# Dilated attention issued for pairs of heads, with their score and value products alternating between the two halves of the TensorE array

## What is computed

```
q, k = rope(a @ w_q[pattern]), rope(a @ w_k[pattern]);  v = a @ w_v[pattern]
s = q k^T / 8, masked to keys of the same residue and inside the window
o_pattern = softmax(s) v;   lse_pattern = max(s) + log(sum(exp(s - max)))
o = sum over the patterns of softmax(lse)_pattern * o_pattern
m = concat(o over the heads) @ w_o
```

## Time and profile before

| | us |
|---|---|
| median of 3 runs | 902.57 |
| lowest and highest run | 902.10, 903.83 |
| span of the profiled execution | 901.5 |
| TensorE busy in it | 873.2 (97%) |
| VectorE busy | 536.8 (60%) |
| ScalarE busy | 473.9 (53%) |
| GpSimd busy | 60.0 (7%) |
| attention of group 0, from its first score matmul to the next stage's first matmul | 41.4 |
| attention of group 1, the same | 41.3 |

### The profile page before, as it was taken

The page is one execution under the profiler, slowest core; times in us unless marked ns, Lnnn a source line. Parts: engine busy times, 40 slices in busy tenths (PEclk is TensorE's granted clock), DMA queues, the critical chain, the costliest instruction groups (busy, mean ns, idle before and its releaser), DMA issues. The chain is left out here.

```text
span 901.5 us, 12726 instructions
## 1 busy us (share of the span) xinstructions
PE 873.2 (97%) x4345; PEld 710.1 (79%) x4345; DVE 536.8 (60%) x1119; ACT 473.9 (53%) x819; POOL 60.0 (7%) x134
## 2 busy tenths in 40 slices
PE   6999999999999999989999999999999999999995
PEld 5898666778888888778887888888788788888874
DVE  5878776587645545685555535545555865555533
ACT  7676666665444444455445544445554644444331
POOL 3000038020000000110000000000001100000002
PEclk9999999999999999999999999999999999999998
DMA  7666100454656456347555015555204376645611
GB/s 251 206 203 222 47 2 1 140 165 157 217 187 222 150 189 226 98 151 241 178 182 158 1 48 173 184 168 187 82 1 141 118 232 199 220 154 188 217 47 48
DMA packets 90107, 135.20 MB, mean 150 GB/s; under 512 B 6304, under 2 KB 55504, under 8 KB 90064
## 3 DMA queue, kind: packets, MB, share of 16 engines
q1 hardware_dynamic: 89392, 132.53, 45.9%
q0 software_dynamic: 576, 2.10, 0.7%
q10 hardware_dynamic: 96, 0.02, 0.0%
HBM read 133.59 MB, written 1.05 MB: 149 GB/s over the span
## 5 line engine op out<-in xcount | busy, mean ns | idle before, releaser
L948 DVE TENSOR_TENSOR w_lo<-w_raw,w_hi 128x1024 fp32r<-128x1024 f32 x248 | 301.3, 1246 | 111.5 <-ACT w_hi L524 107.7
L1377 PE MATMUL ps<-w_hi,xt_hi 128*128 128x512 f32 x784 | 314.5, 401 | 2.1 <-DVE xt_lo L978 1.9
L1377 PE MATMUL ps<-w_hi,xt_lo 128*128 128x512 f32 x784 | 307.4, 392 | 0.0
L1377 PE MATMUL ps<-w_lo,xt_hi 128*128 128x512 f32 x784 | 306.9, 391 | 0.0
L524 ACT ACTIVATE w_hi<-w_raw 128x1024 fp32r<-128x1024 f32 x248 | 252.2, 1054 | 42.5 <-DMA w_raw<-in_ffn_w_gu 19.6
L1377 PEld LDWEIGHTS ps<-w_hi,xt_hi 128*128 128x128 f32 x784 | 148.4, 189 | 32.4 <-DVE xt_lo L978 2.7
L1377 PEld LDWEIGHTS ps<-w_hi,xt_lo 128*128 128x128 f32 x784 | 148.3, 189 | 31.4
L1377 PEld LDWEIGHTS ps<-w_lo,xt_hi 128*128 128x128 f32 x784 | 148.7, 190 | 28.3
L776 ACT ACTIVATE st_hi<-ps 128x256 fp32r<-128x256 f32 x44 | 16.8, 383 | 112.6 <-PE ps L1386 112.6
L1377 PE MATMUL ps<-w_hi,st_hi 128*128 128x512 f32 x176 | 69.0, 392 | 2.9 <-DVE st_lo L1240 2.8
L502 POOL TENSOR_TENSOR h<-h,tmp 128x512 f32<-128x512 f32 x16 | 24.1, 1527 | 714.6 <-DVE tmp L1216 714.6
(11 more groups left out here) (176 smaller groups left out, 825.5 us busy)
## 6 DMA issues: line engine op xcount, KB each, us to landing
w_raw<-in_ffn_w_gu SPq DMA_DIRECT2D x88, 512.0 KB, 4.7
w_raw<-in_dil_w_in SPq DMA_DIRECT2D x72, 512.0 KB, 4.0
w_raw<-in_ffn_w_down SPq DMA_DIRECT2D x44, 512.0 KB, 4.0
w_raw<-in_nsa_w_in SPq DMA_DIRECT2D x20, 512.0 KB, 4.6
w_raw<-in_nsa_w_o SPq DMA_DIRECT2D x8, 512.0 KB, 4.4
w_raw<-in_dil_w_o SPq DMA_DIRECT2D x8, 512.0 KB, 4.0
w_raw<-in_nsa_cmp_wk SPq DMA_DIRECT2D x4, 512.0 KB, 5.2
w_raw<-in_nsa_cmp_wv SPq DMA_DIRECT2D x4, 512.0 KB, 4.0
```

The lines of the kernel that those rows point to most:

```text
L948: dve.tensor_tensor(w_lo[:, n.slot, c:c + 1024], w_raw[:, n.raw, c:c + 1024], w_hi[:, n.slot, c:c + 1024].bitcast(F32), ALU.subtract)\
L1377: ins = pe.matmul(o, s, m, start=start, stop=stop)
```

## The change

Units are walked in pairs: pair t of a group is the units w = 16 hg + 2t (even head) and 16 hg + 2t + 1 (odd head) of the same half m = t % 2, where j = 2 (t // 2) + odd. A unit's number therefore stands for another head and half than before. The three score matmuls and the four value matmuls of the two units are issued alternately, even then odd, each still two instructions. The transposes are not interleaved. The order on the three engines becomes, for step t of eight pairs:

```diff
+        def pair_units(hg, t):
+            return 16 * hg + 2 * t, 16 * hg + 2 * t + 1
...
 ScalarE
-                for s in range(16 + 4):
-                    if 3 <= s < 19:
-                        pt_evac(1, 16 * hg + s - 3, 512)
-                    if s < 16:
-                        exp_unit(1, 16 * hg + s, 512, 1)
-                    if hg == 1 and s in (1, 5, 14):
+                for t in range(8 + 2):
+                    if t >= 2:
+                        for w in pair_units(hg, t - 2):
+                            pt_evac(1, w, 512)
+                    if t < 8:
+                        for w in pair_units(hg, t):
+                            exp_unit(1, w, 512, 1)
+                    if hg == 1 and t in (0, 2, 7):
...
 VectorE
-                for s in range(16 + 1):
-                    if s < 16:
-                        mask_unit(1, 16 * hg + s, 512, [mask_dil[:, s % 2, :]])
-                    if s >= 1:
-                        norm_unit(1, 16 * hg + s - 1, 512, [None])
-                    if hg == 1 and s in (2, 6, 15):
+                for t in range(8 + 1):
+                    if t < 8:
+                        for w in pair_units(hg, t):
+                            mask_unit(1, w, 512, [mask_dil[:, t % 2, :]])
+                    if t >= 1:
+                        for w in pair_units(hg, t - 1):
+                            norm_unit(1, w, 512, [None])
+                    if hg == 1 and t in (1, 3, 8):
...
 TensorE
-            def scores_dil(hg, u):
-                j, m, w = u // 2, u % 2, 16 * hg + u
-                if w >= 3:
-                    pe.wait_ge(masked[1], w - 2)
+            def scores_pair_dil(hg, t):
+                m, ws = t % 2, pair_units(hg, t)
+                for w in ws:
+                    if w >= 3:
+                        pe.wait_ge(masked[1], w - 2)
                 for pat, c, k0, n in ((0, 0, 0, S), (1, 256, m * P, P), (2, 384, m * P, P)):
-                    ins = pe.matmul(bank(score_bank(w), c, n), qk(pat, 0, j, m * P, P), qk(pat, 1, j, k0, n),
-                                    start=True, stop=True)
-                ins.then_inc(scores[1], 1)
+                    for odd, w in enumerate(ws):
+                        j = t // 2 * 2 + odd
+                        ins = pe.matmul(bank(score_bank(w), c, n), qk(pat, 0, j, m * P, P),
+                                        qk(pat, 1, j, k0, n), start=True, stop=True)
+                        if pat == 2:
+                            ins.then_inc(scores[1], 1)
...
+            def pv_pair_dil(hg, t):
+                m, ws = t % 2, pair_units(hg, t)
+                if (hg, t) == (1, 4):
+                    pe.wait_ge(ot_ready[1], 1)
+                pe.wait_ge(pt_out[1], ws[1] + 1)
+                c = ot_bank(hg, t // 4) * 512 + t // 2 % 2 * S + m * P
+                for k, (pat, mk) in enumerate(((0, 0), (0, 1), (1, m), (2, m))):
+                    for odd, w in enumerate(ws):
+                        j = t // 2 * 2 + odd
+                        ins = pe.matmul(view(ps, c, [[1, P]], p0=DH * odd, n=DH),
+                                        v_dil[:, pat, mk, j * DH:(j + 1) * DH],
+                                        p_t[:, w % 4, P * k:P * k + P], start=k == 0, stop=k == 3)
+                if t % 4 == 3:
                     ins.then_inc(pv_done[1], 1)
...
-                for s in range(16 + 5):
-                    if s < 16:
-                        scores_dil(hg, s)
-                    if 3 <= s < 19:
-                        turn_probs(1, 16 * hg + s - 3, 4)
-                    if s >= 5:
-                        pv_dil(hg, s - 5)
+                for t in range(8 + 3):
+                    if 2 <= t < 10:
+                        for w in pair_units(hg, t - 2):
+                            turn_probs(1, w, 4)
+                    if t < 8:
+                        scores_pair_dil(hg, t)
+                    if t >= 3:
+                        pv_pair_dil(hg, t - 3)
```

More of the change, by code:

```diff
@@ L915, in _ @@
                     dil_proj(hg, it + k, Piece(N_DIL + 18 * hg + 6 * k + AHEAD, it))
-                for s in range(16 + 4):
-                    if 3 <= s < 19:
-                        pt_evac(1, 16 * hg + s - 3, 512)
-                    if s < 16:
-                        exp_unit(1, 16 * hg + s, 512, 1)
-                    if hg == 1 and s in (1, 5, 14):
-                        ot_dil(*{1: (0, 0), 5: (0, 1), 14: (1, 0)}[s])
+                for t in range(8 + 2):
[6 more added lines that the diff above has]
+                    if hg == 1 and t in (0, 2, 7):
+                        ot_dil(*{0: (0, 0), 2: (0, 1), 7: (1, 0)}[t])
             ot_dil(1, 1)
@@ L1357, in _ @@
                     dve.wait_ge(dilmask_ready, 1)
-                for s in range(16 + 1):
-                    if s < 16:
-                        mask_unit(1, 16 * hg + s, 512, [mask_dil[:, s % 2, :]])
-                    if s >= 1:
-                        norm_unit(1, 16 * hg + s - 1, 512, [None])
-                    if hg == 1 and s in (2, 6, 15):
-                        ot_dil(*{2: (0, 0), 6: (0, 1), 15: (1, 0)}[s])
+                for t in range(8 + 1):
[6 more added lines that the diff above has]
+                    if hg == 1 and t in (1, 3, 8):
+                        ot_dil(*{1: (0, 0), 3: (0, 1), 8: (1, 0)}[t])
             ot_dil(1, 1)
@@ L1803, in pv_dil @@
-            def pv_dil(hg, u):
-                j, m = u // 2, u % 2
-                if (hg, u) == (1, 8):
-                    pe.wait_ge(ot_ready[1], 1)
[L1807 to L1812, removed]
+            def scores_pair_dil(hg, t):
[3 more added lines that the diff above has]
+                        pe.wait_ge(masked[1], w - 2)
+                for pat, c, k0, n in ((0, 0, 0, S), (1, 256, m * P, P), (2, 384, m * P, P)):
+                    for odd, w in enumerate(ws):
[4 more added lines that the diff above has]
+                            ins.then_inc(scores[1], 1)
```

## The result

The changed kernel takes 897.42 us (median of 5 runs, 895.89 to 900.11) against 902.91 us of the kernel before beside it: ratio 0.9943, 95% interval 0.9928 to 0.9959. The prediction was 894.4, range 891.5 to 898.5. The profiled execution has a span of 894.2 us (predicted 893.3); its time of 895.89 us is the shortest of the five, so the spans differ by 7.3 us where the medians differ by 5.5.

A forecast was written before the change was run, and what follows sets the result against it. TensorE bounds the kernel before; afterwards a closed wait of 4.48 us per pair makes each attention stage 37.3 us, not 41.4. Saving 8.2 from 901.5 gives span 893.3; the median lies 1.07 above, 894.4, range 891.5 to 898.5.

The forecast's parts named there:

- Bound now: Kernel before: TensorE, busy 873 of 901.5 us, bounds it; nothing waits long for VectorE or ScalarE.
- Do the halves overlap?: Attention scores and values: row halves and column halves run at full rate side by side while both have work queued.
- The first rival: Attention stages: halves don't overlap in this order; 3.7 us per stage more than before, median 910; chance 8%.
- the second, that only row halves overlap: Attention values: a pair's products don't overlap and take 1.89 us; median 899.6; chance 5%.
- TensorE per pair: Attention loop: transposes 1.02, scores 1.07 and values 1.02 us, together 3.1 against 5.36 before.
- The new wait: Attention loop: TensorE's transposes wait for norms queued behind both masks of the next pair; 4.48 us per pair.
- the chain: Attention loop: closed circle of scores, two masks, two norms, transposes, next scores; 4.48 us per pair against 5.36.
- mask to mask: VectorE: time from a pair's first mask to its second, taken as 0.77 us within the 4.48 us period.
- The clock: TensorE's 1.4 us pause per pair leaves the clock up; at 1.2 GHz the median would be about 920, chance 2%.
- the granted clock at 1.00: Attention stages: sign that the prediction is right, TensorE's granted clock staying at 1.00 despite its pauses.
- the sum for the stage: One attention stage, first score matmul to next stage's first matmul: 37.3 us against 41.4, with six periods of 4.48.
- Behind the stage: Projections after an attention stage keep TensorE busy 104.7 of 105.6 us, so saved time isn't lost waiting for weights.

The follow-up runs named there:

- e4: Kernel before, with VectorE doing norm(s-1) ahead of mask(s): 905.52 us, ratio 1.0016 to the kernel before.
- e7: Changed kernel, VectorE doing norms of pair t-1 before masks of pair t, and the value products not alternated: 881.95 us, ratio 0.9749 to the kernel before.
- e1: Changed kernel, with VectorE doing the norms of pair t-1 before the masks of pair t: 876.15 us, ratio 0.9691 to the kernel before.
- e3: Changed kernel plus 14 identity transposes in each of steps 2 and 3 of each group, filling TensorE's pauses: 894.28 us, ratio 0.989 to the kernel before.
- e6: Changed kernel with the pauses of steps 2 and 3 filled by identity transposes and scores and values not alternated: 895.39 us, ratio 0.9899 to the kernel before.
- e2: Changed kernel with the alternation of scores and values undone, even head's instructions before the odd head's: 902.87 us, ratio 0.9989 to the kernel before.
- e8: Changed kernel measured again, unedited: 897.39 us, ratio 0.9926 to the kernel before.
- e9: Changed kernel plus 14 identity transposes in step 2 of each group only, filling the first pause: 893.57 us, ratio 0.9903 to the kernel before.
- e10: Changed kernel plus 14 identity transposes in step 3 of each group only, filling the second pause: 896.04 us, ratio 0.9916 to the kernel before.

## Why the prediction was right, and where it was off

**Bound now.** Right. TensorE was full before, and e4 shows that an earlier norm bought nothing there.

**Do the halves overlap?** Right, read from three bursts of the trace before. Twelve scores in 1.15 us and sixteen values in 1.09 are the whole of it. The first rival (no overlap in this order, slower) falls with that. So does the second, that only row halves overlap: sixteen value products, which all use the 128 rows, last no longer than eight. Even in e7, with the values of a pair in order, 16 took 1.58 us and not 1.96. The Trainium skill's page "TensorE: Matmul & The Clock Gate", Part 3, "What overlaps and what doesn't", lets a weight load overlap running matmuls only when its row group differs; for these float32 products the traces disagree.

**TensorE per pair.** 3.1 predicted, 3.13 in e1, the only run that shows it. In the changed kernel it doesn't set the period.

**The new wait.** Right as a mechanism, and e1 shows it: opening the chain and nothing else brings the period from 4.32 to 3.13. The chain's length was forecast at 4.48. The mis-sized term is mask to mask: 0.77 by the one place in the earlier trace rows where two masks follow each other, but the second one waited there for its scores, which end at about 491.47 + 1.14 + 0.87 = 493.48 (an estimate from the earlier trace rows), and it starts at 493.50. Working without a pause it is 0.61 to 0.62 (509.87, 510.49, 511.10). Twelve periods at 0.16 too much are 1.9 us.

**The clock.** This is the step that failed, and with it the sign "the granted clock at 1.00": the stages had 0.91 and 0.95. The prediction took the pause of the steady loop, 1.4 us, set it beside 1.01 us ahead of the stage, let the clock stay, and gave the fall 2%, as a case in which it would be at 1.2 GHz throughout. It didn't look at the steps in which the value products, the cover named for the pause, do not exist yet: there the pause is 2.0 us, and the clock falls for a few us at a time, twice in group 0's stage of the profiled execution and once in group 1's. By e3 that costs 3.1 us of the median and most of the scatter. In the steady loop of pairs, with 0.97 us of pause, no profiled execution has the beginning of a fall, so that half of the argument held. That the length of the pause decides is not shown, as the last section says; that filling these two pauses keeps the clock up is.

The two errors have opposite signs. With the period at 4.32 a stage would have come to 37.3 - 6 x 0.16 = 36.3 us, and e3, the changed kernel without falls, has 36.2 twice: the sum for the stage is then right to 0.1 us. The forecast of the whole would have been 894.4 - 1.9 = 892.5, and its range, moved along, would have ended at 896.6. The measured 897.4 lies outside that. So the mechanism was right, but that the measured time fell inside the range is in part luck: the period, too long by 0.16, made room for the clock that had been left out. As it stands, the forecast is 3.0 us short, the gain 5.5 and not 8.2 us. (The 1.07 us between span and median belong to two different executions. In every run on record the time lies 1.7 to 1.8 us above the span of the same run.)

**Behind the stage.** Right: the projections take 105.7 us, TensorE is full in them, and nothing was given back, nor behind group 1.

**What the name of the change suggests.** I ascribed the gain to pairs and alternation together and didn't part them. The experiments do, with the queues in the order of this change. At full clock the walk in pairs alone gains 902.7 - 895.4 = 7.3 us (e6) and the alternation 1 to 2 more (e3). With the clock as it is, pairs alone gain nothing that could be told from none (e2), so that all of the measured 5.5 us hang on the alternation; most of what it gives there is that the clock stays low for a shorter time.

## What to carry to other kernels

When work is regrouped into larger steps, write down for each engine what stands in front of what in its queue, and follow the circle: a faster engine is worth only what the longest circle lets through, and one exchange of two independent blocks in another engine's queue (here 21 us, 3 of them by the clock) may be worth more than the change itself. The same exchange in the kernel before, which had no such circle, bought nothing (e4). If two engines wait for each other and both have idle time, look for such an exchange before anything else. Look at the first and last steps of a pipeline by themselves, since what covers a wait in the middle isn't there at the ends.

## What was not expected of the hardware

- Pauses of 2.0 us in TensorE went with falls of the granted clock from 1.00 to 0.50, 3.4 us long in most cases, and made the runs of one kernel spread over 4 to 7 us. Fourteen transposes of the identity, 1.75 us, in each pause prevented that (e3, e6). But the length of a pause alone doesn't tell. Of the twelve open pauses of 2.0 us in the profiled executions of the changed kernel, e8, e9 and e10, nine have a fall between 0.2 us ahead of their end and 1.4 us behind it, two have none (the first one of group 1, in the changed kernel and in e8), and one found the clock low already. In e2 a fall began in a pause of 1.46 us, in e8 one behind pauses of 1.01 and 0.87, in e4 one with none over 0.43 close ahead of it. Pauses of 0.97 us in every pair of the steady loop had none. What decides stays open here.
- The value products of two heads in order, one head in each column half, overlapped in part by themselves (e7): 16 instructions in 1.58 us, where eight alone take 1.09 and a second eight in sequence would add 0.87. In e7's trace the starts from 504.40 on form two rows with steps of 0.11 us; the second row begins at 504.89, when the first still has three starts to come, the last at 505.21. That the second row is the odd head's is a reading of this spacing. Weight loads of the second row start beside the running products of the first.
- That the alternation lengthens no latency: the even head's last score is ready as early among twelve alternating instructions as it was among six. The mask starts 509.87 - 508.69 = 1.18 us behind the scores in the changed kernel and 509.18 - 508.00 = 1.18 before.
